# The first expert step's rows leave the one-hot product already turned

## The chip, the cores and the metric

The kernel runs on one core of a Trainium2 chip. The metric is the device time of one execution in microseconds (us); of several executions the median is taken. TensorE (PE in the profile, its weight loads PEld), VectorE (DVE), ScalarE (ACT), GpSimd (POOL) and SyncE (SP) run side by side and wait for one another through semaphores.

## The reference, cut to what matters

Two layers over 384 tokens of width 1024: one tile of 128 context tokens and two tiles of 128 latent tokens. Each layer runs a mixer and then a mixture of 16 experts in 4 groups. All is float32. The part around the change:

```python
g_idx = jnp.argmax(g_logits, axis=-1)                 # one group of four per token
top_v, top_i = lax.top_k(e_sel, TOP_K)                # two experts of that group
w_k = jax.nn.softmax(top_v, axis=-1) * g_w            # gate weights
...
hid = jax.nn.silu(h @ w1[e]) * (h @ w3[e])            # 1024 -> 256, for each expert e
y = y + gate * (hid @ w2[e])                          # 256 -> 1024
...
```

`g_w` is the softmax probability of the chosen group. With two experts left, the first weight is 1 / ((1 + e^(second - first)) * sum of the group exponentials), the second that number times e^(second - first).

## The kernel before, in words

**Expert steps.** The experts of a layer run in steps of 128 rows: 64 rows for each of two neighbouring experts (a pair). Eight pairs need 8 to 19 steps, as the routing has it; ten in either layer here. In a step TensorE multiplies the turned rows (`hTe`, 1024 x 128, the stationary side, 64 columns for each expert) with `w1` and `w3` (L1396), turns the next step's rows (L1383) and the hidden values (L1411), and multiplies with `w2` (L1421). GpSimd gathers the rows of the step after next from `h_rows` in HBM (L427) and scatters finished rows to `y_rows` (L433).

**Weights.** SyncE loads them in a ring of eight places of 2 MB, in a fixed order (L387); each place has a list of what must be done before it is written. The last place lies over `turned` and over tiles 1 and 2 of `xn`; its load waits for the router's matmuls, for the rows' copy to `h_rows` and, in layer 0, for the first step's one-hot product (L235).

**Before step 0.** `rank_tokens` counts tokens per expert. VectorE builds `first_hot` (L889), a one-hot matrix of 384 tokens by 128 places for the first pair, adds the shift to the last tile of `xn` (L893), and then runs the routing chain L896 to L916: small instructions, each waiting for the one before it through a semaphore (`link`). Next to it TensorE picks the first step's rows: `first_rows` multiplies `first_hot` (stationary) with `xn` (moving, 512 wide) into banks 6 and 7 (L1352). ScalarE and VectorE copy one half each to `ys` (L625, L976), TensorE turns `ys` in eight transposes (L1383), and both engines copy the turned halves to `hTe` (L622, L958). A wide matmul whose result nobody reads (`keep_clock`, L1329) stands ahead of `first_rows` and another ahead of the transposes.

**Step contents.** After its copy VectorE writes the step table (L924 to L929), works out the gate weights in four small instructions (L931 to L935) and the right-hand side L936. TensorE's twelve matmuls of `step_contents` (L1373) wait for L936. From their result VectorE makes the row numbers (`of_rows`, L946), on which the first gather waits; the first expert step follows on TensorE.

A float32 matmul shows in the trace as two MATMULs, each with its own weight load; a transpose shows as one.

Of the kernel before, what the change touches and what calls it, by code (L numbers as in the profile page):

```python
# [7 lines left out]
ALU = mybir.AluOpType  # L8
ACT = mybir.ActivationFunctionType
AX = mybir.AxisListType.X  # L10

P = 128
D = 1024
DC = D // P
TILES = 3
# [9 lines left out]
NSLOT = 12  # L25
# [23 lines left out]
def program(nc, x_prompt, x_sample, cache_ckv, cache_kpe, c, c_ctx, mod_w, mod_b, norm1_g, norm2_g,  # L49
# [3 lines left out]
    with ExitStack() as ctx:  # L53
# [5 lines left out]
        def S(name):  # L59

            if name not in sems:
                sems[name] = ctx.enter_context(nc.semaphore(name))
            return sems[name]
# [9 lines left out]
        def L(k, name, n):  # L73

            if name in ROUTE:
                return S("route"), len(ROUTE) * k + ROUTE.index(name) + n
            return S(name), TIMES[name] * k + n
# [9 lines left out]
        xn = sb("xn", [P, TILES, D])  # L87
# [23 lines left out]
        h_rows = nc.dram_tensor("h_rows", (T, D), F32, kind="Internal").ap()  # L111
        ps = ctx.enter_context(nc.psum_tensor("ps", [P, 8, 512], F32))
# [37 lines left out]
        hg = scratch(0, D)  # L150
# [79 lines left out]
        def expert_places(l, order):  # L230

            waits, fills = [], list(count)
            for s in order:
                used = {}
                for o in (owner[s], owner[s + 1]) if s < NSLOT else ((("router_mm", 3 * (l + 1)), ("h_rows", 16 * TILES * (l + 1)), (("first_mm", 2), ("L1_gathered", 16))[l])[0:s - NSLOT + 1]):  # L235
                    used[o[:-1]] = max(used.get(o[:-1], 0), o[-1])
                waits.append(used)
            for n in range(3 * PAIRS):
                s = order[n % RING_PAIRS]
                count[s] += 2  # L240
                owner[s] = owner[s + 1] = (KINDS[n % 3], l, step_entry(n // 3))
            return order, waits, fills
# [70 lines left out]
        class Chain:  # L313
# [5 lines left out]
            def link(self, ins):  # L319
                self.n += 1  # L320
                ins.then_inc(self.sem, 1)
                self.eng.wait_ge(self.sem, self.n)
# [5 lines left out]
        def bank2(b, n):  # L328

            return ps[:, b:b + 2, :].rearrange("p b n -> p (b n)")[:, 0:n]  # L330
# [232 lines left out]
        def _(act):  # L563
# [54 lines left out]
            def experts(l):  # L618
                def turned_tokens(j):

                    act.wait_ge(S(f"L{l}_x_tr"), j + 1)
                    a_.activation(hTe[:, 0:512], ps[:, 2, :], ACT.Copy).then_inc(S(f"L{l}_hTe"), 1)  # L622

                act.wait_ge(S("first_mm"), 2 * l + 1)
                a_.activation(ys[:, 0:512], ps[:, 6, :], ACT.Copy).then_inc(S("first_act"), 1)  # L625
                turned_tokens(0)
                act.wait_ge(*L(l, "table", 1))
                n = act.value_load(table[0:1, l, T_ALL:T_ALL + 1], min_val=PAIRS, max_val=STEPS - 1)
                with act.Fori(0, n) as j:
                    act.wait_ge(S(f"L{l}_gate_mm"), j + 1)  # L630
                    a_.activation(sil, ps[:, 0, 0:DE], ACT.Silu).then_inc(S(f"L{l}_silu"), 1)
                    act.wait_ge(S(f"L{l}_hid_tr"), j + 1)
                    a_.activation(hidT, ps[:, 6, 0:DE].rearrange("p (c n) -> p c n", c=2), ACT.Copy) \
                        .then_inc(S(f"L{l}_hidT"), 1)
                    turned_tokens(j + 1)
                but_last = act.value_load(table[0:1, l, T_BUT_LAST:T_END], min_val=PAIRS - 1, max_val=STEPS - 1)
                act.wait_ge(S(f"L{l}_stored"), but_last * 16)
                for t in range(TILES):
                    for k in range(2):
                        act.dma_start(yg[k][:, t * D:(t + 1) * D], y_rows[l][k * T + t * P:k * T + (t + 1) * P, :]) \  # L640
                            .then_inc(S(f"y_rows{t}"), 16)
# [109 lines left out]
        def _(dve):  # L751
# [115 lines left out]
            def place_tokens(l):  # L867
# [27 lines left out]
                most, rounds = (pairs[:, m, :] for m in range(2))  # L895
                link(v_.tensor_reduce(most, ps[:, 5, 48:64].rearrange("p (q e) -> p q e", e=2), AX, ALU.max))  # L896
                over = (P, PAIRS, T // HALF)
                link(v_.tensor_tensor(past, most.unsqueeze(2).broadcast_to(over), limits[:, 0:T // HALF].unsqueeze(1).broadcast_to(over), ALU.is_gt))
                link(v_.tensor_reduce(rounds, past, AX, ALU.add))
                twice = (P, PAIRS, 2, PAIRS)  # L900
                link(v_.tensor_tensor(so_far, rounds.unsqueeze(1).unsqueeze(1).broadcast_to(twice), earlier.unsqueeze(2).broadcast_to(twice), ALU.mult))
                link(v_.tensor_reduce(steps_at.rearrange("p (q e) -> p q e", e=2), so_far, AX, ALU.add))
                link(v_.scalar_tensor_tensor(R["ranks"], steps_at.unsqueeze(1).broadcast_to((P, TILES, NE)), float(HALF),
                                             ps[:, 5, 0:48].rearrange("p (t n) -> p t n", t=TILES), ALU.mult, ALU.add))
# [14 lines left out]
            def step_contents(l):  # L919

                bs, steps_now = (P, TILES, 2, STEPS), steps_hot[:, :, :, 0:STEPS]
                rhs = R["steps_rhs"].rearrange("p t (v k n) -> p t v k n", v=2, k=2)
                numbers = cst[:, C_TOK:C_HALF].rearrange("p (t k) -> p t k", k=2)
                v_.tensor_tensor(rhs[:, :, 0], steps_now, numbers.unsqueeze(3).broadcast_to(bs), ALU.mult)  # L924
                rounds, s1 = pairs[:, 1, :], steps_at[:, ::2]
                v_.tensor_copy(table[:, l, T_CUM:T_CUM + PAIRS], s1)
                v_.tensor_copy(table[:, l, T_ROUNDS:T_BUT_LAST], rounds)
                v_.scalar_tensor_tensor(table[:, l, T_BUT_LAST:T_END], s1[:, PAIRS - 1:], -1.0, rounds[:, PAIRS - 1:], ALU.add, ALU.add)
                v_.tensor_tensor(table[:, l, T_ALL:T_ALL + 1], s1[:, PAIRS - 1:], rounds[:, PAIRS - 1:], ALU.add).then_inc(S("route"), 1)  # L929
                dve.wait_ge(*L(l, "exps", 1))  # L930
                link(v_.tensor_reduce(R["gsum"], R["gexp"], AX, ALU.add))  # L931
                dve.wait_ge(*L(l, "exps", 2))
                link(v_.scalar_tensor_tensor(R["den"], R["eexp"], 1.0, R["gsum"], ALU.add, ALU.mult))
                link(v_.reciprocal(R["weights"][:, :, 0:1], R["den"]))
                link(v_.tensor_tensor(R["weights"][:, :, 1:2], R["weights"][:, :, 0:1], R["eexp"], ALU.mult))  # L935
                v_.tensor_tensor(rhs[:, :, 1], steps_now, R["weights"].unsqueeze(3).broadcast_to(bs), ALU.mult).then_inc(S("route"), 1)  # L936

            def contents_out(l):
# [15 lines left out]
            def experts(l):  # L954
                def turned_tokens(j):

                    dve.wait_ge(S(f"L{l}_x_tr"), j + 1)
                    v_.tensor_copy(hTe[:, 512:D], ps[:, 3, :]).then_inc(S(f"L{l}_hTe"), 1)  # L958
# [13 lines left out]

                    v_.tensor_tensor(out, bank2(4, D), gates, ALU.mult).then_inc(S(f"L{l}_ys"), 1)  # L973

                dve.wait_ge(S("first_mm"), 2 * l + 2)
                v_.tensor_copy(ys[:, 512:], ps[:, 7, :]).then_inc(S("first_dve"), 1)  # L976
                step_contents(l)
                turned_tokens(0)
                contents_out(l)
                dve.wait_ge(*L(l, "meta", 1))  # L980
                dve.sem_inc(S(f"L{l}_ys"), 1)
# [250 lines left out]
        def _(pe):  # L1232
# [93 lines left out]
            def keep_clock(bank, *widths):  # L1326

                for n in widths:
                    mm(ps[:, bank, 0:n], ident, cst[:, C_CS2:C_CS2 + n], start=True, stop=True)  # L1329
# [10 lines left out]
                             R["mask"][:, s:s + 1, :].broadcast_to((P, after, NE)), start=s == 0, stop=s == TILES - 1)  # L1340
                ins.then_inc(S("rank_mm"), 1)

            def first_rows(l):

                keep_clock(1, 256)
                pe.wait_ge(S("h_made"), 2 * (l + 1))
                pe.wait_ge(*L(l, "first_hot", 1))
                for half in range(2):
                    for t in range(TILES):
                        if (half, t) == (0, TILES - 1):  # L1350
                            pe.wait_ge(S("h_last"), l + 1)
                        ins = mm(ps[:, 6 + half, :], first_hot[:, t, :], xn[:, t, half * 512:(half + 1) * 512],  # L1352
                                 start=t == 0, stop=t == TILES - 1)
                    ins.then_inc(S("first_mm"), 1)

            def last_rows(l, n):

# [19 lines left out]
            def experts(l):  # L1377
                halves = [slice(e * HALF, (e + 1) * HALF) for e in range(2)]

                def turn_rows(chunks, rows=hg):  # L1380

                    for cc in chunks:
                        ins = tr(bank2(2, D)[:, cc * P:(cc + 1) * P], rows[:, cc::DC], ident)  # L1383
                        if cc == DC - 1:
                            ins.then_inc(S(f"L{l}_x_tr"), 1)

# [35 lines left out]
                                         start=cc == 0, stop=cc == 1)  # L1422
                    ins.then_inc(S(f"L{l}_down_mm"), 1)

                first_rows(l)
                keep_clock(1, 384)
                pe.wait_ge(S("first_act"), l + 1)
                pe.wait_ge(S("first_dve"), l + 1)
                turn_rows(range(DC), ys)
                step_contents(l)  # L1430
                for pair in range(PAIRS):
                    pair_arrived(pair, 0)
# [300 lines left out]
```

## Time and profile before

| | |
|---|---|
| median of 3 runs | 752.13 us (750.79 to 753.05) |
| profiled execution, first to last instruction (span) | 748.4 us |
| PE busy / PEld busy | 685.6 us (92%) / 387.9 us (52%) |
| DVE / ACT / POOL busy | 246.5 / 142.0 / 165.4 us |
| DMA | 219.46 MB, mean 293 GB/s |
| chain that ended last | PE 73%, DMA 16%, DVE 6%, issue 2%, ACT 2% |

The profiled execution's own time is known from its first to its last instruction, 748.4 us; the medians also hold what lies around that, 3.7 us by the difference. In the rows below a row of the timeline merges consecutive instructions of one line: start, duration from the first start to the last end, engine, line, tiles, shape, count, and in brackets the idle time just before with what ended it. A wait that the profile puts down to nothing it shows reads <-issue. A TensorE instruction's recorded length includes time in which the next one already runs, so the spacing of a group is its duration less the length of its last instruction, over the count less one. PEclk is the granted clock: 1.00 is 2.4 GHz, 0.50 is 1.2 GHz.

### The profile page before, as it was taken

Reading aid. Unit: us, or ns where it says so; the run is one execution under the profiler, and the core shown is the slowest. Engines: PE = TensorE matmul, PEld = TensorE weight load, DVE = VectorE, ACT = ScalarE, POOL = GpSimd, SP = SyncE. Lnnn points to the kernel's source line nnn. Section 1 sums busy time; section 2 is a strip of 40 time slices with the busy share of each in tenths; the row PEclk is TensorE's granted clock in tenths of the full one; section 3 lists DMA queues with packets and bytes.
Section 4 is the critical chain, followed back from the end, with each engine's and each line's share of the span. In section 5 each row is a group of like instructions: output and inputs, shape, how many; then the busy total and the mean of one; then the engine's idle time right before and its main releaser. Section 6 shows DMA issues by size and latency. Waiting matters only on the chain.

```text
span 748.4 us, 9564 instructions
## 1 busy us (share of the span) xinstructions
PE 685.6 (92%) x3667; PEld 387.9 (52%) x3667; DVE 246.5 (33%) x525; ACT 142.0 (19%) x291; POOL 165.4 (22%) x221
## 2 busy tenths in 40 slices
PE   1799999999999999899989999899899999999990
PEld 0344444564565666556444454356445566666650
DVE  0200312211237223223551423555312733232346
ACT  2100100000221212112132110555112122121201
POOL 5000111011331122212111100357223122222202
PEclk9899999999989999999999999999999899999996
DMA  9999999299539999998580685904501969989842
GB/s 336 394 363 345 381 410 388 82 404 424 244 143 394 407 423 421 420 422 351 198 324 2 249 332 186 376 2 184 183 1 41 409 269 417 421 358 421 332 174 100
DMA packets 53207, 219.46 MB, mean 293 GB/s; under 512 B 13773, under 2 KB 20941, under 8 KB 33968
## 3 DMA queue, kind: packets, MB, share of 16 engines
q1 hardware_dynamic: 31520, 178.59, 59.7%
q0 software_dynamic: 9664, 23.41, 8.3%
q10 hardware_dynamic: 11984, 16.92, 6.5%
q8 instruction: 27, 0.44, 0.2%
q14 instruction: 12, 0.10, 0.0%
HBM read 206.53 MB, written 20.68 MB: 304 GB/s over the span
## 4 chain that ended last, share of the span: by engine, by line
PE 73%; DMA 16%; DVE 6%; issue 2%; ACT 2%; POOL 0%; SPq 0%; ACTq 0%; POOLq 0%; DVEq 0%
PE ps L1396 13%; PE ps L1310 11%; PE ps L1468 7%; PE ps L1421 6%; DMA pool<-in_mod_w 5%; PE ps L1504 5%; PE ps L1245 4%; DMA pool<-in_moe_w 4%; DMA pool<-h_rows,of_now 4%; PE ps L1455 3%; PE ps L1485 3%; PE ps L1638 3%; PE ps L1563 2%; PE ps L1298 2%; PE ps L1383 2%
## 5 line engine op out<-in xcount | busy, mean ns | idle before, releaser
L1396 PE MATMUL ps<-pool 128*64 128x256 f32 x928 | 103.6, 379 | 2.2 <-issue 2.1
L1396 PEld LDWEIGHTS ps<-pool 128*64 128x64 f32 x928 | 76.5, 137 | 31.5 <-issue 9.5
L1310 PE MATMUL ps<-pool,turned 128*128 128x512 f32 x192 | 84.6, 595 | 0.0
L1245 PE MATMUL ps<-pool,cs 128*32 128x512 f32 x384 | 48.3, 630 | 18.5 <-DMA pool<-in_mod_w 9.7
L1468 PE MATMUL ps<-turned,pool 128*128 128x384 f32 x192 | 65.1, 492 | 0.0
L1310 PEld LDWEIGHTS ps<-pool,turned 128*128 128x128 f32 x192 | 35.7, 190 | 41.3 <-issue 41.1
L1421 PE MATMUL ps<-pool 128*64 128x512 f32 x240 | 54.8, 597 | 1.9 <-DMA pool<-in_moe_w 0.8
L1468 PEld LDWEIGHTS ps<-turned,pool 128*128 128x128 f32 x192 | 36.8, 196 | 30.9 <-issue 8.9
L964 DVE SCALAR_TENSOR_TENSOR pool<-ps,pool 128x256 f32<-128x256 f32 x20 | 9.7, 484 | 113.0 <-PE ps L1396 113.0
L417 POOL TENSOR_SCALAR rstd<-ss 128x1 f32<-128x1 f32 x24 | 10.6, 441 | 160.1 <-ACT xn L583 119.6
L547 POOL TENSOR_SCALAR pool<-pool 128x384 f32<-128x384 f32 (+1 forms) x30 | 30.5, 1031 | 59.3 <-DVE pool L1159 59.2
L1504 PE MATMUL ps<-pool,turned 128*128 128x512 f32 (+1 forms) x96 | 37.9, 553 | 1.7 <-ACT turned L597 1.7
L1396 PE MATMUL ps<-turned,pool 128*64 128x256 f32 x272 | 39.4, 379 | 0.0
L583 ACT ACTIVATE xn<-x 128x1024 f32<-128x1024 f32 x15 | 15.8, 1055 | 117.3 <-DVE x L818 85.4
L973 DVE TENSOR_TENSOR pool<-ps,xn 128x1024 f32<-128x1024 f32 x20 | 24.5, 1225 | 37.3 <-PE ps L1421 37.3
L1245 PEld LDWEIGHTS ps<-pool,cs 128*32 128x32 f32 x384 | 10.9, 113 | 48.2 <-issue 27.3
L1421 PEld LDWEIGHTS ps<-pool 128*64 128x64 f32 x240 | 18.8, 136 | 27.6 <-issue 26.5
L427 POOL DMA_INDIRECT pool<-h_rows,of_now x18 | 29.6, 1647 | 15.0 <-POOL of_now L423 15.0
L1396 PEld LDWEIGHTS ps<-turned,pool 128*64 128x64 f32 x272 | 27.5, 137 | 9.7 <-issue 2.6
L817 DVE TENSOR_TENSOR xn<-ps,ga 128x512 f32<-128x512 f32 x12 | 8.3, 691 | 73.7 <-PE ps L1310 59.5
L1383 PE MATMUL ps<-cst,pool 128*128 128x128 f32 x176 | 28.7, 287 | 2.8 <-DMA pool<-h_rows,of_now 1.4
L1383 PEld LDWEIGHTS ps<-cst,pool 128*128 128x128 f32 x176 | 23.1, 194 | 12.0 <-DMA pool<-h_rows,of_now 6.0
(245 smaller groups left out, 899.7 us busy)
## 6 DMA issues: line engine op xcount, KB each, us to landing
pool<-in_moe_w SPq DMA_DIRECT2D x72, 1024.0 KB, 15.1
pool<-in_mod_w SPq DMA_DIRECT2D x24, 2048.0 KB, 12.6
turned<-in_moe_w SPq DMA_DIRECT2D x18, 1024.0 KB, 14.4
pool<-in_ev_w_in SPq DMA_DIRECT2D x6, 1024.0 KB, 20.0
y_rows<-pool ACTq DMA_DIRECT2D x8, 768.0 KB, 20.2
xn<-in_moe_w SPq DMA_DIRECT2D x6, 1024.0 KB
pool<-y_rows ACTq DMA_DIRECT2D x12, 512.0 KB, 6.6
pool<-in_ev_w_in SPq DMA_DIRECT2D x2, 2048.0 KB, 23.1
```

Source lines behind the costliest of these rows:

```text
L427: nc.gpsimd.indirect_dma_start(out=hg, out_offset=None, in_=h_rows[:, :], in_offset=bass.IndirectOffsetOnAxis(ap=index, axis=0), bounds_ch ...
L547: ins = nc.gpsimd.tensor_scalar(probs(h, t), probs(h, t), pinv[:, h % 2, t:t + 1], None, ALU.mult)
L973: v_.tensor_tensor(out, bank2(4, D), gates, ALU.mult).then_inc(S(f"L{l}_ys"), 1)
L1245: ins = mm(ps[32 * j:32 * j + 32, 7, :], cs32[:, 2 * part + c, :], w[:, c, j * 512:(j + 1) * 512], start=part + c == 0, stop=part + c == 4)
L1310: ins = mm(ps[:, 2 * t + n, :], yT[:, k, t * P:(t + 1) * P], weight(parts[k // 4], 4, D)[:, k % 4, n * 512:n * 512 + 512], start=k == 0, s ...
L1383: ins = tr(bank2(2, D)[:, cc * P:(cc + 1) * P], rows[:, cc::DC], ident)
L1396: ins = mm(ps[m, k, 0:DE], hTe.rearrange("p (c n) -> p c n", c=DC)[:, cc, m], w[e][:, cc, :], start=cc == 0, stop=cc == DC - 1)
L1421: ins = mm(ps[m, 4 + n, :], hidT[:, cc, m], w2[e][:, cc, n * 512:n * 512 + 512], start=cc == 0, stop=cc == 1)
L1455: ins = mm(ps[:, t, :], hT[:, cc, t * P:(t + 1) * P], weight("v", DC, 512)[:, cc, :], start=cc == 0, stop=cc == DC - 1)
L1468: ins = mm(ps[:, (3, 0)[j % 2] + k, 0:T], weight(f"{name}.{j // 2}", DC, 256)[:, cc, j % 2::2], hT[:, cc, :], start=cc == 0, stop=cc == DC ...
L1485: mm(ps[:, bu, 0:T], weight("u", DC, 512)[:, cc, g * P:(g + 1) * P], hT[:, cc, :], start=cc == 0, stop=cc == DC - 1)
L1504: ins = mm(ps[:, b, 0:hi - lo], hT[:, cc, t * P:(t + 1) * P], w[:, k, lo:hi], start=cc == 0, stop=cc == DC - 1)
```

## The change

`first_rows` becomes `first_turned`: for each of three token tiles, eight matmuls take 128 columns of `xn` (every eighth column) as the stationary side and `first_hot` as the moving side, and add up in banks 2 and 3. What stands there is the turned matrix, so the copies to `ys`, the `keep_clock` of 384 columns and the eight transposes go. ScalarE copies both halves to `hTe`. VectorE's four instructions for the gate weights move from `step_contents` to places between the links of the routing chain, without links of their own. In layer 0 the last weight place waits for the new product's semaphore.

```diff
-(("first_mm", 2), ("L1_gathered", 16))[l])[0:s - NSLOT + 1]
+(("L0_x_tr", 1), ("L1_gathered", 16))[l])[0:s - NSLOT + 1]
...
-                act.wait_ge(S("first_mm"), 2 * l + 1)
-                a_.activation(ys[:, 0:512], ps[:, 6, :], ACT.Copy).then_inc(S("first_act"), 1)
-                turned_tokens(0)
+                act.wait_ge(S(f"L{l}_x_tr"), 1)
+                for half in range(2):
+                    a_.activation(hTe[:, half * 512:(half + 1) * 512], ps[:, 2 + half, :], ACT.Copy).then_inc(S(f"L{l}_hTe"), 1)
...
+                dve.wait_ge(*L(l, "exps", 2))
+                v_.tensor_reduce(R["gsum"], R["gexp"], AX, ALU.add)
                 link(v_.tensor_tensor(past, ...))
+                v_.scalar_tensor_tensor(R["den"], R["eexp"], 1.0, R["gsum"], ALU.add, ALU.mult)
                 link(v_.tensor_reduce(rounds, past, AX, ALU.add))
+                v_.reciprocal(R["weights"][:, :, 0:1], R["den"])
                 link(v_.tensor_tensor(so_far, ...))
+                v_.tensor_tensor(R["weights"][:, :, 1:2], R["weights"][:, :, 0:1], R["eexp"], ALU.mult)
...
-                dve.wait_ge(*L(l, "exps", 1))
-                link(v_.tensor_reduce(R["gsum"], R["gexp"], AX, ALU.add))
-                dve.wait_ge(*L(l, "exps", 2))
-                link(v_.scalar_tensor_tensor(R["den"], R["eexp"], 1.0, R["gsum"], ALU.add, ALU.mult))
-                link(v_.reciprocal(R["weights"][:, :, 0:1], R["den"]))
-                link(v_.tensor_tensor(R["weights"][:, :, 1:2], R["weights"][:, :, 0:1], R["eexp"], ALU.mult))
...
-                dve.wait_ge(S("first_mm"), 2 * l + 2)
-                v_.tensor_copy(ys[:, 512:], ps[:, 7, :]).then_inc(S("first_dve"), 1)
                 step_contents(l)
-                turned_tokens(0)
...
-            def first_rows(l):
+            def first_turned(l):
                 keep_clock(1, 256)
                 pe.wait_ge(S("h_made"), 2 * (l + 1))
                 pe.wait_ge(*L(l, "first_hot", 1))
-                for half in range(2):
-                    for t in range(TILES):
-                        if (half, t) == (0, TILES - 1):
-                            pe.wait_ge(S("h_last"), l + 1)
-                        ins = mm(ps[:, 6 + half, :], first_hot[:, t, :], xn[:, t, half * 512:(half + 1) * 512],
-                                 start=t == 0, stop=t == TILES - 1)
-                    ins.then_inc(S("first_mm"), 1)
+                for t in range(TILES):
+                    if t == TILES - 1:
+                        pe.wait_ge(S("h_last"), l + 1)
+                    for cc in range(DC):
+                        ins = mm(bank2(2, D)[:, cc * P:(cc + 1) * P], xn[:, t, cc::DC], first_hot[:, t, :],
+                                 start=t == 0 and cc % 4 == 0, stop=t == TILES - 1 and cc % 4 == 3)
+                ins.then_inc(S(f"L{l}_x_tr"), 1)
...
-                first_rows(l)
-                keep_clock(1, 384)
-                pe.wait_ge(S("first_act"), l + 1)
-                pe.wait_ge(S("first_dve"), l + 1)
-                turn_rows(range(DC), ys)
+                first_turned(l)
                 step_contents(l)
```

## Rows read from the trace of the kernel before

**Rows 1.** Chain that ended last, in order of time: start us, us, what.
```profile
229.05 5.40 PE ps L1352 x12
...
292.86 31.96 DMA pool<-in_moe_w
...
600.27 7.13 PE ps L1396 x64
```

**Rows 2.** Timeline of the stretch before step 0 of layer 0.
```profile
234.13 0.29 DVE L916 TENSOR_TENSOR pool<-cst,pool 128x126 f32<-128x126 f32 x1
...
234.54 0.69 DVE L976 COPY pool<-ps 128x512 f32<-128x512 f32 x1
235.15 0.27 DVE L924 TENSOR_TENSOR pool<-pool,cst 128x120 f32<-128x120 f32 x1
...
235.38 1.13 PE L1383 MATMUL ps<-cst,pool 128*128 128x128 f32 x8 [0.30 <-DVE pool L976]
...
235.63 0.16 DVE L931 TENSOR_REDUCE pool<-pool 128x3 f32<-128x12 f32 x1
...
236.43 0.28 DVE L936 TENSOR_TENSOR pool<-pool 128x120 f32<-128x120 f32 x1
236.55 0.60 ACT L622 ACTIVATE pool<-ps 128x512 f32<-128x512 f32 x1 [4.05 <-PE ps L1383]
...
236.76 1.53 PE L1373 MATMUL ps<-pool 128*128 128x40 f32 x12 [0.25 <-DVE pool L936]
...
238.00 0.62 SPq L387 DMA_DIRECT2D xn<-in_moe_w  x1
...
238.55 7.13 PE L1396 MATMUL ps<-pool 128*64 128x256 f32 x64 [0.25 <-issue]
...
239.89 1.12 POOL L427 DMA_INDIRECT pool<-h_rows,of_rows  x1 [7.87 <-DVE of_rows L946]
```

**Rows 3.** Timeline, router of layer 0: links with an instruction between, then without.
```profile
223.28 0.20 DVE L842 TENSOR_TENSOR pool<-pool,cst 128x48 f32<-128x48 f32 x1
...
223.60 0.19 DVE L845 TENSOR_REDUCE pool<-pool 128x12 f32<-128x48 f32 x1
...
224.88 0.21 DVE L842 TENSOR_TENSOR pool<-pool,cst 128x48 f32<-128x48 f32 x1
225.12 0.20 DVE L845 TENSOR_REDUCE pool<-pool 128x12 f32<-128x48 f32 x1
```

**Rows 4.** Timeline, matmuls with 128 stationary and 128 moving columns.
```profile
151.38 0.83 PE L1488 MATMUL ps<-pool 128*128 128x128 f32 x6
```

**Rows 5.** The same line's durations in ns (min/median/max), all its instructions.
```profile
L1488 PE MATMUL ps<-pool x24: 272/275/275, 151.4 to 169.4; 128*128 128x128 f32 x24
```

**Rows 6.** DMA issues from 591 to 594 us: KB each, median us to landing.
```profile
h_rows<-xn POOLq DMA_DIRECT2D x1, 512.0 KB, 6.0
```

**Rows 7.** Timeline of TensorE, layer 0, its two long waits.
```profile
315.17 7.21 PE L1396 MATMUL ps<-pool 128*64 128x256 f32 x64 [1.83 <-issue]
...
324.86 3.65 PE L1421 MATMUL ps<-pool 128*64 128x512 f32 x16 [0.83 <-DMA pool<-in_moe_w]
```

**Rows 8.** DMA issues from 241 to 243 us.
```profile
pool<-in_moe_w SPq DMA_DIRECT2D x2, 1024.0 KB, 7.7
```

**Rows 9.** DMA issues from 290 to 294 us.
```profile
pool<-in_moe_w SPq DMA_DIRECT2D x2, 1024.0 KB, 29.4
```

**Rows 10.** Windows: us, busy of PE, PEld, DVE, ACT, POOL, PEclk, DMA share, GB/s.
```profile
220.14:226.97 6.83, 6.83 (x20) 4.46 (x20) 4.81 (x27) 0.77 (x3) 0.00 (x0) 0.50 1.00 397
...
238.00:240.00 2.00, 1.75 (x17) 1.23 (x18) 0.83 (x6) 0.77 (x1) 0.11 (x1) 1.00 0.78 197
...
312.50:325.50 13.00, 10.29 (x82) 6.12 (x80) 3.14 (x4) 2.18 (x4) 1.67 (x4) 1.00 1.01 418
...
600.00:607.00 7.00, 6.91 (x64) 4.73 (x65) 2.14 (x8) 0.81 (x2) 1.53 (x1) 1.00 0.24 48
```

**Rows 11.** Waits of TensorE from 580 to 748 us, the one for a transfer in an expert step.
```profile
PE ps L1383 <- DMA pool<-h_rows,of_now: 0.5, 1, 0.5
```

More of the change, by code:

```diff
@@ L234, in expert_places @@
                 used = {}
-                for o in (owner[s], owner[s + 1]) if s < NSLOT else ((("router_mm", 3 * (l + 1)), ("h_rows", 16 * TILES * (l + 1)), (("first_mm", 2), ("L1_gathered", 16))[l])[0:s - NSLOT + 1]):
+                for o in (owner[s], owner[s + 1]) if s < NSLOT else ((("router_mm", 3 * (l + 1)), ("h_rows", 16 * TILES * (l + 1)), (("L0_x_tr", 1), ("L1_gathered", 16))[l])[0:s - NSLOT + 1]):
                     used[o[:-1]] = max(used.get(o[:-1], 0), o[-1])
@@ L1378, in experts, with turn_rows @@
                 halves = [slice(e * HALF, (e + 1) * HALF) for e in range(2)]
-                def turn_rows(chunks, rows=hg):
+                def turn_rows(chunks):
                     for cc in chunks:
-                        ins = tr(bank2(2, D)[:, cc * P:(cc + 1) * P], rows[:, cc::DC], ident)
+                        ins = tr(bank2(2, D)[:, cc * P:(cc + 1) * P], hg[:, cc::DC], ident)
                         if cc == DC - 1:
```

## The prediction

> **What bounds the kernel now.** I read four views in this order: the page's chain shares, the chain in order of time, the timeline of the stretch that the change touches, and the windows of the DMA.
>
> The page puts 73% of the chain that ended last on TensorE, 16% on DMA, 6% on VectorE. In time the chain passes the edited stretch in both layers: TensorE's one-hot product at 229.05, then the wait for L936, then L1373 [rows 1, 2]. The reader is to see that TensorE does not decide there. From 234.45 on (229.05 + 5.40, the end of the product) it is VectorE: L916, the copy L976, the table, four linked gate-weight instructions, L936, and only then L1373 on TensorE, 0.05 us after L936 has ended at 236.71 [rows 2]. The transposes end at 236.51 and stand in nobody's way: L1373, queued behind them, waits on L936 for another 0.25 us. Layer 1 repeats the stretch some 361.7 us later (its step 0 starts at 600.27, layer 0's at 238.55).
>
> What comes behind differs between the layers. In layer 1 the DMA is nearly idle while step 0 starts, share 0.24 from 600 to 607 [rows 10], and TensorE waits once in all ten steps for a transfer, 0.5 us for a gather that is itself started from this stretch [rows 11]; the chain stays on TensorE (600.27 and on). So an earlier step 0 there reaches the end. In layer 0 the chain leaves TensorE for a weight load issued at 292.86 and 31.96 us under way [rows 1]. A load issued at 241 to 243 lands after 7.7 us, one issued at 290 to 294 after 29.4 us [rows 8, 9]: the backlog grows, the DMA share is 1.01 at 418 GB/s from 312.5 to 325.5 [rows 10], and TensorE waits 1.83 and 0.83 us, 2.66 us in all, for weights [rows 7]. After 324.86 it runs through to the end of the layer. Layer 0 ends when its bytes have come.
>
> **The change part by part (layer 0's times; layer 1 alike).**
>
> *VectorE up to L936, which decides.* Gone: the copy L976, which holds back L924 by 235.15 - 234.54 = 0.61 us; the four gate-weight instructions with their links, 236.43 - 235.63 = 0.80 us. Added: four instructions without links between links of the chain. Two links with one instruction between them start 223.60 - 223.28 = 0.32 us apart, two without 225.12 - 224.88 = 0.24 us [rows 3], so one costs 0.08 and four cost 0.32 us. Sum: 0.61 + 0.80 - 0.32 = 1.09, taken as 1.1 us. Bounds: wholly hidden, the four cost nothing and the gain is 1.41 us; at the 0.20 us a gate-weight link took (0.80 / 4) they cost 0.80 and it is 0.61 us. I take 0.08, the nearest row (small instructions of the same kind, on the same engine, in the same sort of chain). The new wait for the exponentials costs nothing: in both orders they are from the router, before the one-hot. L936 is then done about 235.6, and L1373 could start at 236.76 - 1.1 = 235.66.
>
> *TensorE up to L1373.* The product becomes 24 matmuls, 48 MATMULs of 128 moving columns, for twelve of 512. L1488 has that shape: six in 0.83 us, the last one 0.275 us long, so a spacing of (0.83 - 0.275) / 5 = 0.111 us [rows 4, 5]. 47 x 0.111 + 0.275 = 5.5 us: end at 234.55, for 234.45 before. That row's stationary side is contiguous; the new one takes every eighth column. The transposes L1383 take their stationary side in the same way and have (1.13 - 0.275) / 7 = 0.122 us [rows 2], which as the upper bound makes 6.0 us, an end at 235.06. Both come before 235.66, so TensorE would idle 0.6 to 1.1 us and the product costs nothing. It begins to count above a spacing of (235.66 - 229.05 - 0.275) / 47 = 0.135 us. The removed `keep_clock` and transposes give nothing by themselves: they lay beside VectorE's chain.
>
> The Trainium skill speaks against this (TensorE: Matmul & The Clock Gate, section "Part 3: Packing small matmuls — row/col tiling"): a weight load overlaps matmuls in flight only where its row group differs. All 48 here use all rows, so by it load and stream add up. The trace disagrees: L1488's spacing of 0.111 us has a load of 128 columns in each. The sum by the row is -1.1 us; by the rule it is the last rival below.
>
> *ScalarE.* Two copies of 0.60 us in a row [rows 2] from about 234.6: `hTe` is whole at 235.85. Step 0 starts behind L1373, 235.66 + 1.53 + 0.26 = 237.45 (238.55 before), so the halving of the engines is hidden with 1.6 us to spare; were that gone, it would cost 0.60 us. What is queued behind the second copy, the table wait and the first SiLU, is due after the gate matmuls.
>
> *GpSimd and SyncE.* The first gather waits for L946, which moves with L1373: 238.79 for 239.89. It also waits for the copy to `h_rows`, which is not moved: in layer 0 it had landed by 238.00, when the load that waits for it went out [rows 2]; in layer 1, issued between 591 and 594 and 6.0 us under way [rows 6], it lands by 600.0 at the latest, and the new gather starts about 600.6. Late in neither. The load of the last weight place in layer 0 waits for the new product instead of the old, 234.55 for 234.45, but goes out at 238.00 for the copy's sake in both; its price is nothing. That is also why the DMA's dip at 238 to 240 (share 0.78) [rows 10] stays.
>
> *Sum.* Layer 1: -1.1 us to the end, bounds -0.6 and -1.4. Layer 0: the steps start 1.1 us sooner, the loads behind the dip arrive when they did, and the 1.83 us wait grows to 2.9: 0. Bounds: -1.1 if the loads move along after all; +0.2 if the earlier gathers and scatters push in front of weights. Span 748.4 - 1.1 = 747.3 us. Around the span lie 752.13 - 748.4 = 3.7 us, so the forecast is 751.0 us, 0.15% below the median before.
>
> **The rivals.**
>
> *Both layers gain.* If in unprofiled runs the weights come a little sooner, layer 0's 2.66 us of waits vanish and it too is bound by TensorE. For: 2.66 us is little beside the 75 us (240 to 315) in which the backlog built up. Against: the landing time that grows from 7.7 to 29.4 us [rows 8, 9]. Time: 752.13 - 2.2 = 749.9 us.
>
> *Nothing.* The four inserted instructions cost their full length, and TensorE's product ends just late enough to eat the rest: 752 us. For: no row has three-element reductions between these links. Against: rows 3.
>
> *Slower by the clock.* TensorE runs at 2.4 GHz here, but from 220.14 to 226.97 it was at 1.2 GHz [rows 10]; ahead of that it had run the router, matmuls 20 columns wide, transposes and gaps. The change takes a wide matmul and eight transposes out of the stretch before step 0. If the clock falls there, step 0 starts at half speed, and a stretch like that one (6.8 us) loses 3.4 us of work: in layer 1 3.4 - 1.1 = +2.3, in layer 0 the waits take up most; 754.4 us. Against: without wide matmuls the stretch is 234.55 to 237.45, 2.9 us; before it was 235.38, where the transposes begin, to 238.55, at least 3.2 us [rows 2], at full clock.
>
> *Slower by the weight loads.* If load and stream add up, the spacing is 0.222 us, the product lasts 10.7 us to 239.75, step 0 starts at 241.54, 3.0 us late. It decides from a spacing of 0.135 us, and from 0.158 us it makes the kernel slower. In layer 1 +3.0, in layer 0 3.0 less the 2.66 us of waits, +0.3: 755.4 us. For: no row shows a two-pass matmul with a strided stationary side and 128 moving columns. Against: rows 4 and the transposes.
>
> **How the numbers follow.** Chances: forecast (layer 1 alone) 0.55, both layers 0.22, nothing 0.10, clock 0.05, weight loads 0.06, 0.02 for the rest. A measurement of this kernel tells 0.3%, 2.3 us, from no change: the three runs before span that much. Faster by more than that means below 749.9: half of "both layers", 0.11, and a tail of the forecast, 0.11, makes 0.22. Slower by more, above 754.4: the weight loads 0.06 and half of the clock, rounded up for the unknown, 0.10. Within: 0.68. The range runs from 749.0 (both layers with the four instructions hidden, 752.13 - 2.8, and some scatter) to 753.0 ("nothing" with the scatter of before); the two slower rivals stay outside.
>
> **What would show it.** Right: no L976 and no transposes before step 0, L1373 starting 1.1 us sooner after the one-hot in both layers, an idle TensorE just before it, the 48 MATMULs within 5.5 to 6.0 us, the step 0 of layer 1 and the end 1.1 us sooner against the start of the product, and in layer 0 a longer wait near 313 to 315 with the same end. Wrong: L1373 released by the product and not by L936; PEclk of 0.50 in step 0; no wait for weights in layer 0; or layer 1's steps waiting for gathers.

## The result and the profile after

The changed kernel takes 758.64 us (754.44 to 763.79, 20 runs) where the kernel before, run beside it, takes 754.38 us (748.01 to 757.94, 20 runs). The ratio of the two is 1.0069 [1.0049, 1.0088]: some 5.2 us slower by the ratio (4.3 by the medians), outside the range and on the other side of the forecast. The profiled execution after has a span of 755.2 us and 757.03 us in all.

The page after, its first part and the chain's shares by engine:

```profile
PE 697.2 (92%) x3719; PEld 405.7 (54%) x3719; DVE 243.2 (32%) x521; ACT 141.7 (19%) x291; POOL 165.4 (22%) x221
...
PE 76%; DMA 12%; DVE 6%; issue 2%; ACT 2%; POOL 1%; SPq 0%; ACTq 0%; POOLq 0%; DVEq 0%
```

TensorE is 11.6 us longer busy (685.6 before), and its weight loads 17.8 us (387.9). VectorE lost 3.3 us. The timeline of the stretch before step 0 of layer 0 in the kernel after, to be set against [rows 2]:

```profile
229.38 11.54 PEld L1348 LDWEIGHTS ps<-pool,xn 128*128 128x128 f32 x48 [0.66 <-issue]
229.41 11.71 PE L1348 MATMUL ps<-pool,xn 128*128 128x128 f32 x48
...
235.10 0.28 DVE L929 TENSOR_TENSOR pool<-pool,cst 128x120 f32<-128x120 f32 x1
235.58 0.28 DVE L935 TENSOR_TENSOR pool<-pool 128x120 f32<-128x120 f32 x1
...
240.95 1.43 PE L1369 MATMUL ps<-pool 128*128 128x40 f32 x12
241.15 1.09 ACT L626 ACTIVATE pool<-ps 128x512 f32<-128x512 f32 x2 [14.62 <-PE ps L1348]
...
241.58 0.43 SPq L387 DMA_DIRECT2D xn<-in_moe_w  x1
242.31 7.13 PE L1392 MATMUL ps<-pool 128*64 128x256 f32 x64
...
243.97 1.46 POOL L427 DMA_INDIRECT pool<-h_rows,of_rows  x1 [11.60 <-DVE of_rows L945]
...
251.96 0.71 PE L1379 MATMUL ps<-cst,pool 128*128 128x128 f32 x4 [2.52 <-DMA pool<-h_rows,of_rows]
```

VectorE does what was forecast: the last instruction ahead of `step_contents` (L935, the old L936) ends 6.45 us after the product's start, 7.66 before, so 1.2 us sooner. It is no longer what TensorE waits for. The product (L1348) lasts 11.71 us for the 5.40 of [rows 2], and L1369 follows it without a wait, 5 us after VectorE has finished. From the product's start to step 0 it is 12.90 us; before it was 238.55 - 229.05 = 9.50.

Layer 1 repeats it (timeline of the kernel after): 12.90 us again, where before it was 9.33 (product at 590.94, step 0 at 600.27).

```profile
595.26 11.71 PE L1348 MATMUL ps<-pool,xn 128*128 128x128 f32 x48 [0.48 <-DVE pool L889]
...
606.80 1.43 PE L1369 MATMUL ps<-pool 128*128 128x40 f32 x12
...
608.16 7.13 PE L1392 MATMUL ps<-pool 128*64 128x256 f32 x64
```

What sets the 11.71 us? The durations of that line (ns, min/median/max), and then windows over both products, with the product's instructions alone (busy of PE, of PEld, granted clock, DMA share, GB/s), both of the kernel after:

```profile
L1348 PEld LDWEIGHTS ps<-pool,xn x96: 312/336/341, 229.4 to 606.4; 128*128 128x128 f32 x96
```

```profile
229.41:232.81 3.40, 3.40 (x14) 3.40 (x15) 0.50 1.04 434
232.81:241.12 8.31, 8.30 (x36) 8.11 (x34) 1.00 0.68 277
595.26:598.04 2.78, 2.78 (x12) 2.78 (x12) 1.00 1.02 430
598.04:601.45 3.41, 3.41 (x16) 3.41 (x16) 0.50 1.01 417
601.45:606.97 5.52, 5.52 (x24) 5.33 (x23) 1.00 0.67 275
```

A load is recorded with 336 ns, where contiguous ones have 190 (shown below). And the pace is the same in all windows, 5.52 / 23 = 0.24 us at 2.4 GHz, 3.41 / 14 to 16 = 0.21 to 0.24 at 1.2 GHz. Something that TensorE's clock does not speed up hands out a load every 0.24 us; 48 of them make the 11.5 us.

The profiled spans differ by 755.2 - 748.4 = 6.8 us. By stretches: layer 0's product starts 0.4 later, the stretch to step 0 takes 3.4 more, from there to layer 1's product 0.6, layer 1's stretch 3.6, its ten steps 0.2, and the tail after them 1.3 less (22.3 for 23.6). These are two single executions; over many the difference is 5.2 us. The shorter tail is not the change's: in the repeat with layer 0 alone, below, layer 1 has the old code and a tail of 22.3 too.

### The profile page after: what moved, and what is told of

Its sections match the earlier page's. It is cut to its first block, busy times and chain, and to the rows that moved or that the text cites. A ratio compares the mean times of both kernels' runs of the same rounds, so it can differ in the third digit from the quotient of the medians.

```text
span 755.2 us, 9660 instructions
## 1 busy us (share of the span) xinstructions
PE 697.2 (92%) x3719; PEld 405.7 (54%) x3719; DVE 243.2 (32%) x521; ACT 141.7 (19%) x291; POOL 165.4 (22%) x221
## 4 chain that ended last, share of the span: by engine, by line
PE 76%; DMA 12%; DVE 6%; issue 2%; ACT 2%; POOL 1%; SPq 0%; ACTq 0%; POOLq 0%; DVEq 0%
PE ps L1392 13%; PE ps L1306 11%; PE ps L1460 8%; PE ps L1417 7%; DMA pool<-h_rows,of_now 6%; PE ps L1496 5%; PE ps L1241 5%; DMA pool<-in_mod_w 3%; PE ps L1447 3%; PE ps L1348 3%; PE ps L1477 3%; PE ps L1630 3%; PE ps L1379 2%; PE ps L1555 2%; PE ps L1613 2%
## 5 line engine op out<-in xcount | busy, mean ns | idle before, releaser
L1306 PEld LDWEIGHTS ps<-pool,turned 128*128 128x128 f32 x192 | 35.8, 190 | 41.2 <-issue 41.1
L1417 PE MATMUL ps<-pool 128*64 128x512 f32 x240 | 56.4, 611 | 1.1
L1379 PE MATMUL ps<-cst,pool 128*128 128x128 f32 x160 | 26.4, 288 | 4.2 <-DMA pool<-h_rows,of_rows 2.5
L1496 PEld LDWEIGHTS ps<-pool,turned 128*128 128x128 f32 x96 | 18.0, 190 | 20.0 <-issue 20.0
```

What stands on the lines that cost most here:

```text
L1306: ins = mm(ps[:, 2 * t + n, :], yT[:, k, t * P:(t + 1) * P], weight(parts[k // 4], 4, D)[:, k % 4, n * 512:n * 512 + 512], start=k == 0, s ...
L1379: ins = tr(bank2(2, D)[:, cc * P:(cc + 1) * P], hg[:, cc::DC], ident)
L1417: ins = mm(ps[m, 4 + n, :], hidT[:, cc, m], w2[e][:, cc, n * 512:n * 512 + 512], start=cc == 0, stop=cc == 1)
L1496: ins = mm(ps[:, b, 0:hi - lo], hT[:, cc, t * P:(t + 1) * P], w[:, k, lo:hi], start=cc == 0, stop=cc == DC - 1)
```

## The experiments

The theory: a float32 weight load whose columns lie 32 bytes apart takes about 0.24 us, whatever the clock. The rivals: a load and its stream of 128 columns add up (the prediction's last rival); adding up over eight regions of two banks is slow; the transfers that run beside the product (DMA share 1.0 in the windows above) slow its reads; the VectorE part of the change does harm; or the clock.

**The rows made contiguous.** As the change, but ScalarE first copies each tile of `xn` so that the 128 columns of a load lie side by side.

```diff
+                    a_.activation(apart[t].rearrange("p (c q) -> p c q", c=DC), xn[:, t, :].rearrange("p (q c) -> p c q", c=DC), ACT.Copy)
...
-                        ins = mm(bank2(2, D)[:, cc * P:(cc + 1) * P], xn[:, t, cc::DC], first_hot[:, t, :],
+                        ins = mm(bank2(2, D)[:, cc * P:(cc + 1) * P], apart[t][:, cc * P:(cc + 1) * P], first_hot[:, t, :],
```

> The changed kernel, but ScalarE first copies each xn tile so that the 128 columns of a stationary side lie next to one another; 24 matmuls, banks, moving side and order as they were. Theory A (a float32 weight load of every eighth column takes 0.24 us whatever else happens): spacing 0.11 us, product 5.5 us for 11.7, L1373's successor starts 6.6 us after the product's start (7.7 before the change, 11.5 after), the time is 1 us below the kernel before (ratio 0.9985, between 0.997 and 1.001). Theory B (load and stream add up, whatever the columns' distance): spacing stays at 0.21 to 0.24, product 10 to 12 us, ratio 1.004 to 1.009 as with the change. Theory C (the accumulation over eight regions of two banks is slow): as B.

Measured: 751.68 us against 754.05, ratio 0.9973 [0.9947, 0.9999]. Its timeline in layer 1:

```profile
591.58 5.88 PE L1351 MATMUL ps<-pool 128*128 128x128 f32 x48 [0.93 <-ACT pool L627]
597.30 0.28 DVE L940 TENSOR_TENSOR pool<-pool 128x120 f32<-128x120 f32 x1
...
597.63 1.53 PE L1372 MATMUL ps<-pool 128*128 128x40 f32 x12 [0.18 <-DVE pool L940]
...
599.25 7.13 PE L1395 MATMUL ps<-pool 128*64 128x256 f32 x64
```

The same 48 loads and streams take 5.88 us, 0.119 us each ((5.88 - 0.275) / 47), and now L1372 does wait for VectorE (L940). Load and stream don't add up, and the eight regions and the transfers (DMA share 1.01 over this product) are the same here: these three rivals fall. In layer 0 the product ran partly at 1.2 GHz (granted clock 0.76) and took 7.22 us: a contiguous product does follow the clock.

**The VectorE part undone.** The change with the four gate-weight instructions back in `step_contents`, with their links.

```diff
                 v_.tensor_tensor(table[:, l, T_ALL:T_ALL + 1], s1[:, PAIRS - 1:], rounds[:, PAIRS - 1:], ALU.add).then_inc(S("route"), 1)
...
+                link(v_.tensor_reduce(R["gsum"], R["gexp"], AX, ALU.add))
...
+                link(v_.scalar_tensor_tensor(R["den"], R["eexp"], 1.0, R["gsum"], ALU.add, ALU.mult))
+                link(v_.reciprocal(R["weights"][:, :, 0:1], R["den"]))
+                link(v_.tensor_tensor(R["weights"][:, :, 1:2], R["weights"][:, :, 0:1], R["eexp"], ALU.mult))
...
```

> The changed kernel with the four gate-weight instructions back behind the step table, linked as before; the turned product stays. If the product alone decides when the step contents start (all theories of a slow product): its end stays 11.5 us after its start, VectorE's L936-like last instruction ends about 0.5 us later and still 5 us before it, ratio equal to the change's within 0.002. Rival, VectorE's chain counts too: 0.5 us more in either layer, ratio 0.0013 above the change's.

Measured: 758.18 us, ratio 1.0053 [1.0024, 1.0081]. The timeline of layer 0:

```profile
229.21 11.68 PE L1349 MATMUL ps<-pool,xn 128*128 128x128 f32 x48
...
235.91 0.28 DVE L936 TENSOR_TENSOR pool<-pool 128x120 f32<-128x120 f32 x1
...
240.73 1.43 PE L1370 MATMUL ps<-pool 128*128 128x40 f32 x12
...
242.09 7.13 PE L1393 MATMUL ps<-pool 128*64 128x256 f32 x64
```

L936 ends 0.5 us later after the product's start (6.98 us for 6.45) and nothing waits for it: step 0 is 12.88 us behind the product's start, as with the change. The VectorE part has no share in the loss that this measurement can tell; the loss goes with the turned product.

**A table of load distances.** The kernel before, with groups of matmuls at its end whose results nobody reads; each group changes one thing. Its total (795.14 us) says nothing.

```diff
+            for k in range(16):
+                mm(ps[:, 7, k % 4 * P:k % 4 * P + P], cst[:, 0:4 * P:4], cst[:, C_CS2:C_CS2 + P], start=True, stop=True)
...
+                    mm(ps[h * HALF:(h + 1) * HALF, 7, k % 4 * P:k % 4 * P + P], cst[:, h * 512:(h + 1) * 512:8], cst[:, C_CS2:C_CS2 + P], start=True, stop=True)
```

> The kernel before, and at its end ten groups of idle matmuls from the constants into bank 7; read are only the groups' spacings, the time means nothing. 128 moving columns and 128 stationary ones at distances of 1, 2, 4, 8, 16 elements; transposes with distance 8; distance 8 with 32 and with 512 moving columns; contiguous stationary with moving columns at distance 8; halves of 64 columns at distance 8. Theory A: 0.11 us at distance 1, 0.24 at 8 and no less with 32 moving columns, 0.43 with 512 (hidden behind the stream); transposes 0.11; somewhere between 1 and 8 it rises, if in proportion to the bytes spanned then 0.24 at 4 or 8 and more at 16. Theory B: 0.21 to 0.24 at every distance, 0.13 with 32 moving columns, 0.53 with 512.

Its timeline: stationary columns at distance 1, 2, 4, 8 and 16; then at distance 8 transposes, a moving side of 32 and one of 512 columns; then a contiguous stationary and a moving side at distance 8 (L1684); then distance 8 in halves of 64 columns (L1687).

```profile
733.10 3.73 PE L1668 MATMUL ps<-cst 128*128 128x128 f32 x32
736.67 3.93 PE L1670 MATMUL ps<-cst 128*128 128x128 f32 x32
740.43 7.63 PE L1672 MATMUL ps<-cst 128*128 128x128 f32 x32
747.90 7.77 PE L1674 MATMUL ps<-cst 128*128 128x128 f32 x32
755.51 7.15 PE L1676 MATMUL ps<-cst 128*128 128x128 f32 x32
762.50 1.91 PE L1678 MATMUL ps<-cst 128*128 128x128 f32 x16
764.25 7.71 PE L1680 MATMUL ps<-cst 128*128 128x32 f32 x32
771.77 9.72 PE L1682 MATMUL ps<-cst 128*128 128x512 f32 x16
781.33 7.62 PE L1684 MATMUL ps<-cst 128*128 128x128 f32 x32
788.88 4.15 PE L1687 MATMUL ps<-cst 128*64 128x128 f32 x64
```

From the start of one group to the next and over the count: 0.11, 0.12, 0.23, 0.24, 0.22 us for distances 1, 2, 4, 8, 16. It is a step between 2 and 4, not a slope. The transposes at distance 8 have 0.11, the price of a contiguous load. A moving side of 32 columns costs as much as one of 128 (0.24): the load alone sets the pace. One of 512 columns hides it: the first six matmuls of that group, at 1.2 GHz, start 0.85 us apart, the others, at 2.4 GHz, 0.43 us, as those of the old product with its contiguous loads do. Neither the DMA nor the clock makes the 0.24: two windows of this run, over the groups of 128 and of 32 moving columns at distance 8 (columns as in [rows 10]), have a DMA share of 0.00, and the second has a granted clock of 0.67:

```profile
747.90:755.50 7.60, 7.60 (x33) 7.60 (x33) 0.00 (x0) 0.00 (x0) 0.00 (x0) 1.00 0.00 1
764.25:771.70 7.45, 7.45 (x34) 7.45 (x32) 0.00 (x0) 0.00 (x0) 0.00 (x0) 0.67 0.00 0
```

The load durations of the groups at distance 1, 4 and 8, in ns:

```profile
L1668 PEld LDWEIGHTS ps<-cst x32: 190/192/193, 732.7 to 736.4; 128*128 128x128 f32 x32
...
L1672 PEld LDWEIGHTS ps<-cst x32: 311/329/330, 740.3 to 747.5; 128*128 128x128 f32 x32
...
L1674 PEld LDWEIGHTS ps<-cst x32: 334/336/337, 747.8 to 755.1; 128*128 128x128 f32 x32
```

**Halves.** The last group of that table cost 0.06 us for 64 columns at distance 8, a quarter of 128 columns' price. So the change with each load cut in two, into the two halves of the output's partitions:

```diff
+                        for h in range(2):
+                            ins = mm(bank2(2, D)[h * HALF:(h + 1) * HALF, cc * P:(cc + 1) * P], xn[:, t, h * 512 + cc:(h + 1) * 512:DC], first_hot[:, t, :],
...
```

> The changed kernel with each stationary side of 128 strided columns split in two of 64, which write partitions 0 to 63 and 64 to 127; nothing is copied. 96 passes for 48. Theory A with one path for all loads: 0.12 us per load of 64 columns, 96 x 0.12 = 11.5 us, ratio as with the change, 1.005 to 1.008. Theory A with a limit on each half of the columns, the two halves loading side by side (L1255 of the kernel before, 32 passes of 64 strided columns in 2.11 us, has 0.066 each): 96 x 0.06 = 5.8 us, the step contents start about 1 us sooner than before, ratio about 0.9985. Theory B (load and stream add up): per pair 0.06 + 0.11 at least, 8 us or more.

Measured: 751.84 us, ratio 0.9965 [0.9934, 0.9995]. With twice the instructions the product takes 7.57 us in this profile, part of it at 1.2 GHz.

To keep the clock up there, a version with a wider idle matmul ahead of the product (`keep_clock(1, 512, 128)` for `keep_clock(1, 256)`), and the first halves again beside it on one chip:

> The two halves side by side, and the idle matmul ahead of the product 512 and 128 columns wide for 256. In the run of the halves TensorE ran at 1.2 GHz for a part of the product in both layers and the product took 7.6 us. If more wide work just ahead of it keeps 2.4 GHz, the product takes 5.9 us, the step contents wait for VectorE, and the time is 0.5 to 1 us below the halves'. If the clock falls all the same, the time is the halves', ratio 0.9965, within what a measurement tells.

> The halves once more, on the same chip as the three others, for the comparison with the wide one and for a second interval against the kernel before: ratio 0.9965 again, between 0.993 and 1.000.

Measured: 750.67 us, ratio 0.998 [0.9953, 1.0007], and 752.3 us, ratio 0.9986 [0.9967, 1.0005]. They can't be told apart, and the unchanged halves had full clock this time too: 6.15 us, with L1370 released by VectorE. So the wide matmul is not shown to do anything. The timeline of the halves run again, layer 1:

```profile
592.72 6.15 PE L1349 MATMUL ps<-pool,xn 128*64 128x128 f32 x96 [0.48 <-DVE pool L889]
...
599.22 1.53 PE L1370 MATMUL ps<-pool 128*128 128x40 f32 x12 [0.35 <-DVE pool L935]
```

**One layer at a time.** The change in layer 0 alone, then in layer 1 alone; the other layer keeps the code of before.

```diff
+        TURNED = (0,)
...
+                if l in TURNED:
+                    first_turned(l)
+                else:
+                    first_rows(l)
```

> The change in layer 0 alone (product turned, copies and transposes gone, gate weights between the links, the last weight place waiting for the product); layer 1 as before. The product ends 6.2 us later than before, the first expert step starts 3.4 us later, and the load of the last weight place goes out about 3.5 us later, since it now waits for the product. If layer 0's weights pin its end and follow that load, the layer ends 3 to 4 us later: ratio 1.004 to 1.005. If the 2.66 us of waits in layer 0 take the delay up, as the prediction had it for a late step 0: ratio 1.000 to 1.002.

> The change in layer 1 alone; layer 0 as before. Step 0 of layer 1 starts 3.4 to 3.6 us later after its one-hot than before, and nothing there gives it back: ratio 1.003 to 1.005. If the tail of the layer (the last rows' way through HBM) takes part of it up, as 4.32 us late at layer 1's product became 6.8 us at the end in the changed kernel: 2.5 us, ratio 1.003.

Measured: 754.61 us, ratio 1.0021 [0.9998, 1.0044], and 753.16 us, ratio 1.0007 [0.9985, 1.003]. Neither is told from no change. The four were repeated together on one chip: the change, each layer alone, and the contiguous version.

> The changed kernel itself, beside its two halves by layer on one chip, since the two layers alone came to 1.0021 and 1.0007 and both together to 1.0069 on another chip. If the two add up: 1.003 here. If both together are more than the sum: 1.006 to 1.007.

> The change in layer 0 alone, once more: 1.002 if the first measurement holds. From the profiles: one-hot to step 0 takes 13.6 us with the change at either clock, and 10.2 to 12.5 us without it, as the clock falls; so 1 to 3.5 us at step 0, of which the waits for weights may take some.

> The change in layer 1 alone, once more: 13.6 us from the one-hot to step 0 for 10.0 (2.4 GHz) to 11.7 us (a part at 1.2 GHz), with nothing behind it to take it up: 2 to 3.5 us, ratio 1.003 to 1.005. The first measurement had 1.0007, up to 1.003.

> The contiguous copies once more: ratio 0.9973 again, between 0.995 and 0.999; profile: one-hot to step 0 of 8.8 us in layer 1 at 2.4 GHz.

Measured, against 753.33 us for the kernel before: 757.39, ratio 1.006 [1.0034, 1.0086]; 754.72, ratio 1.0023 [0.9987, 1.0058]; 754.52, ratio 1.0006 [0.9975, 1.0036]; 750.79, ratio 0.9954 [0.9928, 0.998].

The loss and the contiguous gain repeat. The layers alone add up to about half of the loss of both, though the intervals allow the whole. The profiles show that a layer's loss varies, because the old code's stretch is not always 9.4 us. The timeline of layer 1, old code, in the first run with layer 0 alone, and then in its repeat:

```profile
597.21 7.08 PE L1385 MATMUL ps<-xn,pool 128*128 128x512 f32 x12 [0.48 <-DVE pool L897]
...
608.21 7.13 PE L1429 MATMUL ps<-pool 128*64 128x256 f32 x64
```

```profile
595.55 5.39 PE L1385 MATMUL ps<-xn,pool 128*128 128x512 f32 x12 [0.48 <-DVE pool L897]
...
604.86 7.13 PE L1429 MATMUL ps<-pool 128*64 128x256 f32 x64
```

The first has a granted clock of 0.76 over its product and takes 11.00 us to step 0, the second 9.31. In the first run with layer 1 alone the old product of layer 0 had 0.70, and it took 11.80. The turned product takes 12.9 us in every one of these profiles. So step 0 comes 3.4 to 3.6 us later where the old product has full clock and 1.1 to 1.9 where it has not. That can be why layer 1 alone, whose two intervals end at 2.3 and 2.7 us, stays below the 3.6 us of the profile after; how often the old product runs at less than full clock in executions without a profile is not known. It does not explain why both layers together lose twice the sum, for it would lessen their loss as well.

## Why the prediction was wrong, step by step

*TensorE up to L1373: the step that failed.* The prediction sized the 48 MATMULs at a spacing of 0.111 us, with 0.122 us as the upper bound, and put the change's harmless limit at 0.135 us. It is 0.24 us. L1488 [rows 4, 5] was the right row for the shape and the wrong one for the operand: its columns are contiguous. The prediction saw that, and let the transposes stand in for the strided columns. But the table shows that a transpose at distance 8 costs 0.11 us and a matmul at the same distance 0.24 us. Its argument against the last rival, "rows 4 and the transposes", stood on two rows of which neither was a strided load of a matmul. The kernel before has one such row, L1255, and it would have misled too: its loads are halves of 64 columns, 0.06 us apart. The bound from above should have been taken farther out. Of the prediction's signs of being wrong two came: the product releases L1369, and in layer 0 of this profile TensorE waits for no weights (below).

*The last rival* had the time nearly right, 755.4 us, a product of 10.7 us and step 0 3.0 us late, and gave it 0.06. That is luck, for its mechanism is refuted: contiguous loads and streams overlap (0.11 us at distance 1, 0.119 in the contiguous version), so that the Trainium skill's sentence that a load overlaps matmuls only where the row group differs ("TensorE: Matmul & The Clock Gate", section "Part 3: Packing small matmuls — row/col tiling") is not borne out here. Another section bears on what was seen. The Trainium skill, "SBUF — State Buffer", section "Door 1: The DMA port swizzle (why `[64,N]` ≈ `[32,N]`)", says that consecutive accesses have full bandwidth when at least two of them fall into one line of 16 bytes. The table agrees with that in where the step lies: 8 bytes apart 0.12 us, 16 bytes apart 0.23. It does not agree with that section's other sentence, that a stride of four float32 values is free, if that means a distance of 4 (0.23 us). By the lines alone the transposes should have paid too; a moving side at distance 8 did (L1684, 0.23 us). That the lines are the cause is argued, not shown.

*VectorE up to L936.* Forecast -1.1 us, measured -1.2 (6.45 for 7.66). Its parts: without the link changes it is 6.98, so the copy was worth 0.68 us (0.61 forecast) and the moved instructions 0.53 (0.80 - 0.32 = 0.48 forecast). It decides only where the product is short: in layer 1 of the contiguous version above and in the halves run again.

*ScalarE.* The 1.6 us to spare are gone, because `step_contents` now follows the product directly: the copies end at 242.24, step 0 starts at 242.31 and no wait is shown between. They were just hidden.

*GpSimd and SyncE.* The load of the last weight place was priced at nothing because the copy to `h_rows` held it until 238.00. It now goes out at 241.58, right behind the product. Two windows of the kernel after (busy of PE, PEld, DVE, ACT, POOL, then clock, DMA share, GB/s) follow. In the kernel before, the first has a DMA share of 0.78 [rows 10]; the second stands in the fence behind.

```profile
238.00:240.00 2.00, 2.00 (x11) 2.00 (x10) 0.00 (x0) 0.00 (x0) 0.00 (x0) 1.00 0.25 98
240.00:242.00 2.00, 2.00 (x16) 2.00 (x15) 0.00 (x0) 0.85 (x2) 0.00 (x0) 1.00 0.00 0
```

```profile
240.00:242.00 2.00, 2.00 (x22) 1.38 (x20) 1.41 (x2) 0.00 (x0) 1.00 (x1) 1.00 0.98 393
```

The DMA stands still for some 3 us in the layer of which the prediction said that it ends when its bytes have come. The first gather goes out 4.1 us late too, and TensorE waits for it longer. The waits of TensorE in the kernel after from 225 to 370 us (total, times, longest), and then that gather's wait in the timeline before:

```profile
PE ps L1379 <- DMA pool<-h_rows,of_rows: 2.5, 1, 2.5
PE ps L1333 <- DVE pool L871: 0.7, 1, 0.7
PE ps L1379 <- DMA pool<-h_rows,of_now: 0.5, 2, 0.4
```

```profile
246.42 0.71 PE L1383 MATMUL ps<-cst,pool 128*128 128x128 f32 x4 [0.74 <-DMA pool<-h_rows,of_rows]
```

The wait for this gather is no sure mark of the change: the old code in layer 0 has none in the first run with layer 1 alone and 2.7 us in its repeat.

*The sum.* Layer 1's reasoning held with the other sign: its ten steps take 124.5 to 125.8 us in the profiles of the change, of the kernel before and of the versions with the contiguous rows and the halves, so a shift of step 0 there reaches the end. Layer 0's 0 held as far as seen for an earlier step 0, which did not shorten the layer. From the one-hot to its last rows' product the contiguous version's profile takes 139.7 us, the kernel before 138.8; the wait for the first gather took the gain back (3.19 us there). A later step 0 is another matter. From the product's start to the last rows' product layer 0 takes 138.1 us before and 141.7 after: the 3.4 us arrive whole, where the last rival let the 2.66 us of waits for weights take them up. These waits are gone in this profile (1.4 us in the repeat of the change), but the wait for the first gather is 1.8 us longer, and TensorE is 1.4 us longer busy, with a stretch at 1.2 GHz right behind that wait (a window of the kernel after):

```profile
254.00:256.00 2.00, 2.00 (x6) 0.54 (x4) 1.27 (x2) 1.28 (x1) 1.44 (x1) 0.50 1.01 426
```

In four profiles with the old code in layer 0 this way takes 138.1 to 139.6 us, in five with the change there 140.9 to 145.4. How much of that is the late load, the late gather or the clock was not separated. The rival with the clock is not the cause of the long product, which has one pace at both levels.

*Left open.* Why the layers alone add up to half of the loss of both. And the contiguous version's gain, 0.3 and 0.5%, is more than layer 1's 1.2 us (0.16%), which the first interval allows and the second does not; whether layer 0 gives the rest in executions without a profile was not settled.

*A version that beats both.* The contiguous copy on an idle ScalarE does, in both measurements (0.9973 and 0.9954); it is the change with its one dear operand repaired. The halves did in the first and could not be told from the kernel before in the second.

## What to carry to other kernels

Before turning a product around, look at how each operand is read: the price of a load is that of its access pattern, and a row with the same shape but another pattern or another kind of instruction is no bound. Where a float32 stationary side has its columns four or more apart, hide the load behind a wide stream (512 columns did), load halves of 64 columns that alternate between the two halves of the output's partitions, or make the rows contiguous on an engine that is idle. And when an instruction that was off the path grows, ask again what else its end releases: here it was a 2 MB weight load, which went out 3.6 us later and had been priced at nothing. What it cost was not separated.

## What the hardware showed unexpectedly

- A float32 load of 128 stationary columns: 0.11 us each at distance 1, 0.12 at 2, 0.23 at 4, 0.24 at 8, 0.22 at 16. The 0.24 does not follow TensorE's clock (0.24 in the group with a granted clock of 0.67 too); the contiguous product does (5.88 us at 2.4 GHz, 7.22 with a part at 1.2).
- Transposes at distance 8 pay nothing for it: 0.11 us. Why they differ stays open.
- A moving side at distance 8 with a contiguous stationary one costs as much: 0.23 us for 128 columns (L1684).
- 64 columns at distance 8 cost 0.06 us where the two halves alternate, though one such load is recorded with 212 ns: several are under way at a time.
